# Block 1 of a two-block transformer kernel: rotation moved into the projection, gates into the attention's stage, chunk states scanned in another order, outputs normalised tile by tile

## The chip, the cores and the metric

The kernel runs on one core of one Trainium2 chip. The metric is the device time of one execution in microseconds (us). The engines are called TensorE (PE), VectorE (DVE), ScalarE (ACT), GpSimd (POOL) and SyncE (SP), as in the profile. PE has a clock with two levels, 1.2 and 2.4 GHz; the profile gives the granted clock as a share of the higher one.

## The reference, cut to what matters

The program computes two transformer blocks over 512 latent and 256 context tokens, width 1024, all in float32. Only the token mixer of the first block is touched:

```
q_l = apply_axial_rope(dq_l); k_l = apply_axial_rope(dk_l)
a_l = softmax(q1 k1) v - lam * softmax(q2 k2) v          # 4 heads, differential attention
a_l = rms_norm(a_l, da_subln_g) * (1 - lambda_init)
g_f, g_b = log_gate(lowrank, w2, b)                       # log_sigmoid(...) / 16
# gated linear attention, chunks of 64 tokens, forward and backward:
new_state = state * exp(b_last) + k_to_end^T v
o = (q_dec k_inv^T, masked) v + q_dec state
g_l = rms_norm(o_l, gla_norm_g) * silu(gr_l)
y_lat = concat(a_l, g_l) @ w_out
```

Beside that, the kernel turns the conditioning vectors of all three layers (block 1 and the two layers of block 2) from rows into columns; the later stages need them as columns and, through DRAM, as rows.

## The kernel before

Each engine has its own instruction stream, written by hand. The streams meet at fences: `fence(eng, n)` drains the engine, adds one to the semaphore `stage_done`, and waits until PE, ACT, DVE and POOL have all arrived. SP is not one of the four; it waits for a stage number where it needs one. What lies between two fences is called a stage. The stages of the first block are, in this order:

1. first (loads, modulation of layer 0), 2. `norm1`, 3. `lin1` (the input projection), 4. the modulation's turn and the rotation, 5. attention with its RMS norm, 6. gates, 7. decays (`dec`), 8. states, 9. `glao` (outputs of the linear attention and their norm), 10. `turn` (128x128 transposes), 11. `lin` with `w_out`, 12. norm, 13. routing, then the experts.

**Stage 3, `lin1`.** The weight matrix comes in half blocks x = 0..11 of 512 columns by 512 rows. For each x, ACT rounds the half block to its high part (`act_split1`), DVE makes the low part (`dve_split1`, L590), and PE multiplies four or six token tiles, three matmuls per product. The results are evacuated into `pjt` in turn by ACT and DVE (L715, L718). Columns `DQ` and `DK` (the attention's q and k) are done at x = 3, `GR` (the output gate) comes last, x = 10 and 11. Between the tiles PE works on the modulation of the three layers (L279), DVE copies these out (`dve_mod`, L290), and ACT writes them to DRAM and waits for it (`act_mod`, L298).

**Stage 4.** PE, DVE and ACT turn the modulation (`pe_mod_turn`, `dve_mod_turn` L319 and L326, `act_mod_turn` L331 to L333; ACT waits for its writes to land). Then `dve_da_before` sets two rows to one (L1046), rotates q and k of the four latent tiles, 16 heads of 64 at a time (`dve_rope`, L993 to L998), and sums the products for lambda; ACT takes their exp and DVE makes `lam`. At the same time POOL writes 4 MB of zeros to `ybuf` (L3082) and waits for them to land, and SP loads `x` (2 MB) and `w_out` (4 MB) for stage 11.

**Stage 5.** The attention has 16 units (4 heads by 4 query tiles) in a pipeline over PE, ACT and DVE. After the last one DVE runs `rms_heads`: sums of squares for four tiles, one square root on ACT (L1039), then the scaling by 1/rms and by the gain (L1030, L1035).

**Stage 6.** PE multiplies the low-rank gates by `w2a` (L1091, 33 rows), ACT does Abs, Exp and Ln (L1097, L1100, L1103) and DVE takes `min(x, 0)` minus that (L1110).

**Stage 8.** PE makes the contribution of each of the 12 chunks (chunk 0 to 11), ACT and DVE evacuate them alternately (L1231, L1233), and when all are out DVE scans them, 11 steps of 4 instructions (L1242), forward in the order 8, 9, 10, 11, 0, ..., 7 and backward in 11, 10, 9, 8, 7, ..., 0.

**Stage 9.** For each of four latent tiles PE makes the scores (L1261), DVE masks them (L1295), PE multiplies them by the values and adds the states' part (L1273, L1281), ACT evacuates (L1310). After the fourth tile `rms_heads` runs for all four, ACT takes the Silu of `GR` (L1313), and DVE multiplies by it (L1303).

Of the kernel before, what the change touches and what calls it, by code (L numbers as in the profile page):

```python
# [109 lines left out]
def program(nc, I, out):  # L110
    ctx = ExitStack()
    with ctx:
# [60 lines left out]
        t1_a, t1_v, hi1_a, hi1_v = sem("t1_a"), sem("t1_v"), sem("hi1_a"), sem("hi1_v")  # L173
        w2z, x_again = sem("w2z"), sem("x_again")
# [131 lines left out]
        def pe_mod_turn(pe, layers):  # L306

            for l in layers:
                pe.wait_ge(modr_in[l], 16)
                nc.tensor.transpose(bank(l, 96), modr[0:96, P * l:P * l + P], ident[0:96, 0:96]).then_inc(modT_done, 1)  # L310
            for l in layers:
                pe.wait_ge(modc_ok, l + 1)
                nc.tensor.transpose(bank(3 + l, P)[0:96, :], modc[:, l, :], ident).then_inc(modT_done, 1)

        def dve_mod_turn(dve, layers):
            for i, l in enumerate(layers):
                dve.wait_ge(modT_done, 2 * layers[0] + i + 1)
                b = cols[:, R_MB + 48 * l:R_MB + 48 * l + 48].unsqueeze(1).broadcast_to([P, 2, 48])
                nc.vector.tensor_tensor(modc[:, l, :].rearrange("p (w n) -> p w n", w=2), bank(l, 96).rearrange("p (w n) -> p w n", w=2),  # L319
                                        b, ALU.add).then_inc(modc_ok, 1)  # L320
                dve.drain()
# [6 lines left out]
        def act_mod_turn(act, layers):  # L328
            for i, l in enumerate(layers):
                act.wait_ge(modT_done, 2 * layers[0] + len(layers) + i + 1)  # L330
                act.activation(modr[0:96, P * l:P * l + P], bank(3 + l, P)[0:96, :], ACT.Copy).then_inc(modb_ok, 1)  # L331
                act.wait_ge(modb_ok, l + 1)
                act.dma_start(modd[l].rearrange("w (s q) -> (w s) q", q=P), modr[0:96, P * l:P * l + P]).then_inc(modd_in, 16)  # L333
            act.wait_ge(modd_in, 16 * (layers[-1] + 1))
# [287 lines left out]

        def act_lin1(act, n, p):
            q = 0
            for x in range(N1):
# [13 lines left out]
        def dve_lin1(dve, n, p):  # L639
            q = 0  # L640
            for x in range(N1):
                j, half = x // 2, x % 2
                for m, t in enumerate(BL1[j][2]):
# [9 lines left out]
            nc.vector.tensor_copy(lrt[1][0:32, :], bank(33 % 6, 256)[0:32, :]).then_inc(evac_v, 1)  # L653

# [389 lines left out]
        def dve_da_before(dve):  # L1044
            for r in lrt:
                nc.vector.memset(r[32:33, :], 1.0)  # L1046

            dve.wait_ge(prm, 16 * 7)
            for t in LAT:
                dve_rope(dve, t, hv(DQ, 16, 64)(t), 16, 16, C_R1C, C_R1S, Z[:, 2048 * (t % 2):2048 * (t % 2) + 1024],  # L1050
                         Z[:, 2048 * (t % 2) + 1024:2048 * (t % 2) + 2048])
            l4 = lamt.rearrange("p (a b d) -> p a b d", a=2, b=2)
            pr = Z[:, 9000:9128].rearrange("p (a d) -> p a d", a=2)
# [39 lines left out]
        def act_gates(act, n):  # L1093
# [4 lines left out]
            act.drain()  # L1098
            for b in range(2):
# [106 lines left out]

        def plan_st(n):
            return Plan(n, "av" * 6)

        def pe_states(pe, n):  # L1210
            p = plan_st(n)
            for ci in range(12):
                t, c = ci // 2, ci % 2
                if ci >= 8:
                    pe.wait_ge(EV[p.own[ci - 8]], p.val[ci - 8])
                rs = slice(64 * c, 64 * c + 64)
                for d in range(2):
                    for h in range(4):
                        last = nc.tensor.matmul(bank(ci % 8)[64 * (h % 2):64 * (h % 2) + 64, 256 * d + 128 * (h // 2):256 * d + 128 * (h // 2) + 128],
# [4 lines left out]
        def each_states(eng, n, who):  # L1224
            p = plan_st(n)
            for ci in range(12):
                if p.own[ci] == who:
                    eng.wait_ge(mm_done, p.done(ci))
                    dst = Z[:, 512 * ci:512 * ci + 512]
                    if who == "a":  # L1230
                        nc.scalar.activation(dst, bank(ci % 8), ACT.Copy).then_inc(evac_a, 1)  # L1231
                    else:
                        nc.vector.tensor_copy(dst, bank(ci % 8)).then_inc(evac_v, 1)  # L1233
            if who == "v":
                eng.wait_ge(evac_a, p.val[10])
                eng.drain()
                for s in range(1, 12):
                    for d, order in enumerate((FWD, BWD)):
                        a, b = order[s - 1], order[s]
                        for q in range(2):  # L1240
                            k = 8 * (b // 2) + 4 * d + 2 * q + b % 2
                            nc.vector.scalar_tensor_tensor(DD[:, b, d, q, :], DD[:, a, d, q, :], dec[:, k:k + 1], DD[:, b, d, q, :],  # L1242
                                                           ALU.mult, ALU.add)
                    eng.drain()
# [40 lines left out]

        def dve_glao(dve, n):
            p = plan_o(n)
            for t in range(TL):
# [1973 lines left out]
```

## Time and profile before

| what | value |
|---|---|
| time, median of 3 runs | 4025.27 us (4022.03 to 4025.39) |
| the profiled execution | 4030.13 us, span 4028.2 us |
| PE / DVE / ACT / POOL busy | 3414.9 / 1570.6 / 1107.3 / 647.8 us |
| stages 4 to 10, from the span's start | 325 to 575.5 us |

The profile is of one execution. Times are from the start of its span; an instruction's row gives start, duration, engine, line and operands, and in brackets the idle time of its engine before it and what ended that. "L221" is the fence.

### The profile page before, as it was taken

What the parts mean: (1) busy time and instruction counts of PE and PEld (TensorE: products, weight loads), DVE (VectorE), ACT (ScalarE), POOL (GpSimd) and SP (SyncE); (2) the same over time, 40 slices, a digit from 0 to 9 for tenths busy, and PEclk for the clock granted to TensorE, in tenths of its full rate; (3) what the DMA queues carried; (4) which work ended last, traced back from release to release, by engine and by line L of the source; (5) the groups of instructions that cost most, each with busy time, mean ns of one, the idle gap of its engine ahead of it and who ended that gap; (6) DMA issues with size and microseconds to landing.
All of it is one profiled execution on the core that took longest, in us unless ns stands there. A gap on an engine that the chain in (4) does not pass through costs nothing.

```text
span 4028.2 us, 41123 instructions
## 1 busy us (share of the span) xinstructions
PE 3414.9 (85%) x16083; PEld 2352.7 (58%) x16083; DVE 1570.6 (39%) x2654; ACT 1107.3 (27%) x1925; POOL 647.8 (16%) x471
## 2 busy tenths in 40 slices
PE   4996765787882998788999799999599888988998
PEld 2664543222231884445886488888485456856886
DVE  3226642000004356563333433333474563425444
ACT  3112411112112225443221222221234543303221
POOL 1000001000003325122220100000245223401000
PEclk8998876889996999899999899999799999998999
DMA  6883022799995311002112211111521002233222
GB/s 257 334 314 128 1 105 65 304 427 428 428 429 195 100 44 22 9 1 84 63 63 94 94 63 63 63 63 50 176 81 33 9 35 101 85 110 120 89 93 79
DMA packets 159784, 534.00 MB, mean 133 GB/s; under 512 B 9532, under 2 KB 64724, under 8 KB 136572
## 3 DMA queue, kind: packets, MB, share of 16 engines
q1 hardware_dynamic: 136252, 401.04, 26.9%
q0 software_dynamic: 16880, 92.26, 6.6%
q10 hardware_dynamic: 6480, 38.34, 2.4%
q8 instruction: 116, 1.90, 0.2%
q14 instruction: 56, 0.46, 0.0%
HBM read 488.84 MB, written 42.78 MB: 132 GB/s over the span
## 4 chain that ended last, share of the span: by engine, by line
PE 59%; DVE 4%; ACT 2%; DVEq 1%; DMA 1%; issue 1%; POOL 0%; ACTq 0%; POOLq 0%
PE ps L2774 11%; PE ps L2780 11%; PE ps L1840 7%; PE ps L1842 7%; PE ps L1841 7%; PE ps L511 5%; PE ps L2053 4%; PE ps L2105 2%; PE ps L2093 2%; PE ps L2087 1%; DVE Z L2677 1%; DMA ring<-in_w_out_dram 1%; DVE small L2193 0%; DVE hT_hi L2681 0%; DMA xl<-xspill 0%
## 5 line engine op out<-in xcount | busy, mean ns | idle before, releaser
L2774 PE MATMUL ps<-hT_hi,w_hi 128*128 128x512 f32 (+1 forms) x768 | 275.6, 359 | 27.9 <-DVE w_lo L2828 27.9
L2774 PE MATMUL ps<-hT_hi,w_lo 128*128 128x512 f32 (+1 forms) x768 | 276.4, 360 | 0.0
L2774 PE MATMUL ps<-hT_lo,w_hi 128*128 128x512 f32 (+1 forms) x768 | 275.8, 359 | 0.0
L1840 PE MATMUL ps<-wp_hi,hT_hi 128*128 128x512 f32 (+2 forms) x608 | 222.6, 366 | 37.2 <-POOL wp_lo L1819 37.2
L2780 PE MATMUL ps<-w_hi,h_hi 128*128 128x512 f32 x640 | 253.7, 396 | 0.0
L2780 PE MATMUL ps<-w_hi,h_lo 128*128 128x512 f32 x640 | 253.7, 396 | 0.0
L2780 PE MATMUL ps<-w_lo,h_hi 128*128 128x512 f32 x640 | 253.6, 396 | 0.0
L2053 PE MATMUL ps<-Z 64*128 64x256 f32 (+3 forms) x576 | 202.1, 548 | 28.2 <-DVE small L2195 12.5
L2493 POOL TENSOR_TENSOR mr_lo<-ring,wm_hi 128x2048 fp32r<-128x2048 f32 x36 | 170.7, 4754 | 312.1 <-ACT wm_hi L2485 312.0
L1842 PE MATMUL ps<-wp_hi,hm_lo 128*128 128x512 f32 (+2 forms) x608 | 220.8, 363 | 0.0
L1841 PE MATMUL ps<-wp_lo,hT_hi 128*128 128x512 f32 (+2 forms) x608 | 220.2, 362 | 0.0
L1840 PE MATMUL ps<-wm_hi,hT_hi 128*128 128x512 f32 x480 | 192.6, 401 | 28.3 <-POOL mr_lo L2493 28.3
L2797 ACT ACTIVATE w_hi<-ring 128x2048 fp32r<-128x2048 f32 x64 | 121.9, 1908 | 336.1 <-PE ps L2780 326.7
L511 PE MATMUL ps<-ring,hT 128*128 128x512 f32 x448 | 197.6, 604 | 10.3 <-DMA ring<-in_w_out_dram 9.5
L1605 PE MATMUL ps<-ring,Z 128*64 128x512 f32 x512 | 146.2, 736 | 55.4 <-ACT Z L1627 55.4
L1841 PE MATMUL ps<-mr_lo,hT_hi 128*128 128x512 f32 x480 | 190.7, 397 | 0.0
L1842 PE MATMUL ps<-wm_hi,hm_lo 128*128 128x512 f32 x480 | 190.7, 397 | 0.0
L2828 DVE TENSOR_TENSOR w_lo<-ring,w_hi 128x2048 fp32r<-128x2048 f32 x64 | 146.5, 2292 | 79.9 <-ACT w_hi L2797 79.9
L2774 PEld LDWEIGHTS ps<-hT_hi,w_hi 128*128 128x128 f32 x768 | 145.0, 189 | 52.0 <-issue 28.3
L2850 DVE TENSOR_TENSOR pj<-pj,ps 128x512 f32<-128x512 f32 x140 | 95.5, 686 | 195.0 <-PE ps L2780 195.0
L2774 PEld LDWEIGHTS ps<-hT_lo,w_hi 128*128 128x128 f32 x768 | 145.1, 189 | 24.8
L2774 PEld LDWEIGHTS ps<-hT_hi,w_lo 128*128 128x128 f32 x768 | 145.7, 190 | 23.1
(443 smaller groups left out, 6492.7 us busy)
## 6 DMA issues: line engine op xcount, KB each, us to landing
pj<-in_expert_w_up_dram SPq DMA_DIRECT2D x32, 2048.0 KB, 18.3
pj<-in_expert_w_down_dram SPq DMA_DIRECT2D x32, 2048.0 KB, 19.7
ring<-in_expert_w_gate_dram SPq DMA_DIRECT2D x32, 2048.0 KB, 15.9
ring<-in_ffn_w_dram SPq DMA_DIRECT2D x64, 1024.0 KB, 5.2
ring<-in_w_in_dram SPq DMA_DIRECT2D x58, 1024.0 KB, 5.3
Z<-in_w_mod_dram POOLq DMA_DIRECT2D x24, 2048.0 KB, 8.1
Z<-in_w_ada_dram POOLq DMA_DIRECT2D x8, 2048.0 KB, 9.0
ring<-in_w_out_dram SPq DMA_DIRECT2D x6, 2048.0 KB, 16.2
```

The source lines that it names most:

```text
L511: last = nc.tensor.matmul(bank(i % nb, w), lhs(k, t), s[:, k * w:k * w + w], start=(k == 0), stop=(k == nk - 1))
L1605: last = nc.tensor.matmul(bank(2 + m)[64 * x:64 * x + 64, :], xgT[:, k, 64 * x:64 * x + 64], mslot[2 * m + x][:, 512 * k:512 * k + 512], s ...
L1840: nc.tensor.matmul(out_, a_hi, b_hi, start=first, stop=False)
L1841: nc.tensor.matmul(out_, a_hi, b_lo, start=False, stop=False)
L1842: return nc.tensor.matmul(out_, a_lo, b_hi, start=False, stop=final)
L2053: return nc.tensor.matmul(A.lat(u, x) if k0 == 0 else A.ctx(u, x), S["kq"](p, x, "q")[rs, P * t:P * t + P], S["kq"](p, x, "k")[rs, P * k0: ...
L2493: pool.tensor_tensor(mr_lo[:, 2048 * (x % 4):2048 * (x % 4) + 2048], mring[x % 4], wm_hi[:, 2048 * (x % 3):2048 * (x % 3) + 2048], ALU.sub ...
L2774: last = nc.tensor.matmul(bank(i % 8, c1 - c0), W[a][:, k, :], r[:, k, c0:c1], start=(k == 0 and r is hhk and a == 0), stop=(k == KT - 1 a ...
L2780: last = nc.tensor.matmul(bank(i % 8), H1[hb % 2][a][:, k, P * what:P * what + P], W[b][:, k, :], start=(k == 0 and a == b), stop=(k == 3 ...
L2797: act.activation(WHI[x % 2], raw[x % 4], ACT.Copy).then_inc(w_hi_ok, 1)
L2828: nc.vector.tensor_tensor(WLO[x % 2], raw[x % 4], WHI[x % 2], ALU.subtract).then_inc(w_lo_ok, 1)
L2850: nc.vector.tensor_tensor(y, y, bank(i % 8), ALU.add).then_inc(out_read, 1)
```

## The change

- `dve_rope` for the four tiles is called inside `dve_lin1`, before half blocks x = 4, 5, 6 and 8, as two calls of 8 heads (q, then k); the scratch is the still unused `GR` columns. The products for lambda are summed at the start of `dve_lin1`, ACT's exp is at the start of `act_lin1`, the two rows of ones and `lam` come at the end of `dve_lin1`. Stage 4 as such is gone.
- The modulation's turn and the gates come behind the attention in one stage. On PE the order is attention, gates, turn; on ACT attention, six Abs, the norm's square root, Exp, Ln, turn; on DVE attention, norm, turn, gates. The turn uses one bank each way. ACT no longer waits there for its writes; it waits before it loads the gate row in the `turn` stage.
- The chunks' contributions are made in the order 8, 11, 9, 10, 0, 7, 1, 6, 2, 5, 3, 4, all evacuated by ACT; each scan step waits only for the chunks that it needs. ACT takes Silu of `GR` at the end of that stage.
- POOL multiplies Silu(`GR`) by the gain, one tile per instruction, in the `glao` stage. DVE normalises tile t-1 there after it has masked tile t, with a square root on ACT for each tile.
- POOL's zeros to `ybuf` stay between the third and the fourth fence, now beside the attention. Two fences fewer; the waits of SP on a stage number follow.

```diff
         def dve_lin1(dve, n, p):
             q = 0
+            dve.wait_ge(prm, 16 * 7)
+            dve_lambda_sums(dve)
             for x in range(N1):
                 j, half = x // 2, x % 2
+                if x in ROPE_AT:
+                    if x == ROPE_AT[0]:
+                        dve.wait_ge(evac_a, p.val[8])
+                        dve.drain()
+                    t = ROPE_AT.index(x)
+                    for i, c in enumerate((DQ, DK)):
+                        dve_rope(dve, t, hv(c, 8, 64)(t), 8, 16, C_R1C, C_R1S, pjt[:, 2 * i, GR:GR + 512], pjt[:, 2 * i + 1, GR:GR + 512])
+                    dve.drain()
...
+            for r in lrt:
+                nc.vector.memset(r[32:33, :], 1.0)
+            dve_lambda(dve, n)
...
                 act.activation(sp_[:, t, :], bank(t), ACT.Abs)
             act.drain()
+            rms_heads(act, "a", n, LAT, hv(DQ, 4, 128), 4, 128, subln)
...
+        def dve_states(dve, n):
+            p = plan_st(n)
+            for s in range(1, 12):
+                dve.wait_ge(evac_a, p.val[max(ORD.index(c) for k in range(s + 1) for c in (FWD[k], BWD[k]))])
...
+        def pool_glao(pool):
+
+            for t in LAT:
+                g = hv(GR, 4, 128)(t)
+                pool.tensor_tensor(g, g, glag.unsqueeze(1).broadcast_to([P, 4, 128]), ALU.mult).then_inc(grg_ok, 1)
...
+            def norm(t):
+                v = hv(DK, 4, 128)(t)
+                sq = Z[:, 8192 + 512 * (t % 2):8704 + 512 * (t % 2)].rearrange("p (h d) -> p h d", h=4)
+                ss, vv, sd, rr = (st[:, a + 4 * t:a + 4 * t + 4] for a in (200, 260, 320, 380))
+                dve.wait_ge(evac_a, p.val[6 * t + 5])
+                V.tensor_tensor(sq, v, v, ALU.mult)
+                dve.drain()
+                V.tensor_reduce(ss, sq, AX, ALU.add)
+                dve.drain()
+                V.tensor_scalar(vv, ss, 1.0 / 128, EPS, ALU.mult, ALU.add).then_inc(var, 1)
+                n["std"] += 1
+                dve.wait_ge(std, n["std"])
+                V.reciprocal(rr, sd)
+                dve.drain()
+                V.tensor_tensor(v, v, rr.unsqueeze(2).broadcast_to([P, 4, 128]), ALU.mult)
+                dve.drain()
+                dve.wait_ge(grg_ok, t + 1)
+                V.tensor_tensor(v, v, hv(GR, 4, 128)(t), ALU.mult)
...
             pe_lin1(pe, n)
             fence(pe, n)
-            pe_mod_turn(pe, (0, 1, 2))
-            fence(pe, n)
             pe_attn(pe, n, *da_spec())
-            fence(pe, n)
             pe_gates(pe, n)
+            pe_mod_turn(pe)
             fence(pe, n)
...
             fence(act, n)
+            act.wait_ge(modd_in, 16 * 3)
             load_gate(act, 0, 2)
```

## Rows read from the trace of the kernel before

**Rows 1.** Stretches: their length, busy time of each engine, PE's clock, DMA share.

```profile
core 0: us, PE busy (x) PEld busy (x) DVE busy (x) ACT busy (x) POOL busy (x), PEclk, DMA share, GB/s
72.00:325.00 253.00, 252.23 (x1328) 159.07 (x1328) 59.65 (x68) 32.02 (x35) 22.97 (x32) 0.99 0.81 305
325.00:352.40 27.40, 1.41 (x6) 0.66 (x6) 17.52 (x36) 2.19 (x5) 5.20 (x9) 0.54 0.98 369
352.40:364.80 12.40, 8.93 (x22) 5.23 (x23) 4.70 (x8) 2.77 (x5) 0.00 (x0) 0.50 0.11 43
364.80:447.10 82.30, 76.84 (x436) 57.61 (x434) 72.82 (x149) 41.40 (x84) 0.00 (x0) 1.00 0.00 1
...
459.00:470.00 11.00, 10.60 (x12) 3.83 (x12) 0.00 (x0) 3.30 (x6) 0.00 (x0) 0.50 0.00 0
...
569.00:575.50 6.50, 5.68 (x32) 5.44 (x32) 2.77 (x4) 2.39 (x4) 0.00 (x0) 0.68 0.47 161
```

**Rows 2.** Waits, 324 to 576 us: total, times, longest.

```profile
PE ps L781 <- ACTq L221: 25.0, 1, 25.0
...
DVE Z L960 <- POOLq L221: 7.2, 1, 7.2
```

**Rows 3.** Timeline, DVE at the end of stage 3 and in stage 4.

```profile
324.52 0.41 DVE L653 COPY pj<-ps 32x256 f32<-32x256 f32 x1 [5.61 <-PE ps L1842]
...
325.44 0.26 DVE L319 TENSOR_TENSOR small<-ps,small 128x96 f32<-128x96 f32 x1 [0.51 <-PE ps L310]
...
325.79 0.40 DVE L326 SCALAR_TENSOR_TENSOR small<-small 128x8 f32<-128x8 f32 x4
...
327.65 0.76 DVE L1046 MEMSET pj<- 1x512 f32 x2
328.42 1.22 DVE L993 TENSOR_TENSOR Z<-pj,consts 128x1024 f32<-128x1024 f32 x1
```

**Rows 4.** Timeline, DVE inside the projection.

```profile
165.44 2.79 DVE L290 COPY Z<-ps 2x512 f32<-2x512 f32 x4 [12.40 <-PE ps L279]
...
178.62 0.69 DVE L718 COPY pj<-ps 128x512 f32<-128x512 f32 x1 [0.36 <-PE ps L1842]
...
218.24 2.29 DVE L590 TENSOR_TENSOR w_lo<-ring,w_hi 128x2048 fp32r<-128x2048 f32 x1 [9.21 <-ACT w_hi L582]
```

**Rows 5.** Timeline, end of the attention and the gates, all engines.

```profile
445.45 1.58 PE L832 MATMUL ps<-pj,Z 128*128 128x128 f32 x12 [0.48 <-DVE pj L953]
...
453.07 0.21 ACT L1039 ACTIVATE small<-small 128x16 f32<-128x16 f32 x1 [7.72 <-DVE small L1020]
...
456.47 2.50 DVE L1035 TENSOR_TENSOR pj<-pj,Z 128x512 f32<-128x512 f32 x4
...
469.69 0.60 ACT L1097 ACTIVATE Z<-ps 128x512 f32<-128x512 f32 x1 [1.11 <-PE ps L1091]
470.34 1.28 ACT L1100 ACT_TABLE_LOAD   x1
...
475.84 2.86 ACT L1103 ACTIVATE Z<-Z 128x1536 f32<-128x1536 f32 x2
477.44 3.42 DVE L1110 SCALAR_TENSOR_TENSOR Z<-ps,Z 128x1536 f32<-128x1536 f32 x2 [18.47 <-ACT Z L1103]
```

**Rows 6.** Timeline, DVE in the states and output stages.

```profile
509.90 0.69 DVE L1233 COPY Z<-ps 128x512 f32<-128x512 f32 x1 [1.08 <-PE ps L1219]
...
515.55 13.27 DVE L1242 SCALAR_TENSOR_TENSOR Z<-Z,small 128x128 f32<-128x128 f32 x44
...
543.44 1.42 DVE L1295 TENSOR_TENSOR Z<-ps,consts 128x256 f32<-128x256 f32 x4 [4.28 <-PE ps L1261]
...
554.83 0.69 DVE L1016 TENSOR_TENSOR Z<-pj 128x512 f32<-128x512 f32 x1 [4.28 <-ACT pj L1310]
...
566.36 2.50 DVE L1303 TENSOR_TENSOR pj<-pj 128x512 f32<-128x512 f32 x4
```

**Rows 7.** Groups by line and shape, up to 1300 us: busy us, mean ns.

```profile
L690 POOL TENSOR_TENSOR hm_lo<-pj,hT_hi 128x512 fp32r<-128x512 f32 x8 | 11.5, 1453 | 52.0 <-ACT hT_hi L682 51.3 <-DVE hT_hi L703 0.7
```

More of the change, by code:

```diff
@@ L326, in dve_mod_turn, with act_mod_turn @@
                         nc.vector.scalar_tensor_tensor(Ac[:, l, w, m, :], s, 1.0, g, ALU.add, ALU.mult)
[L328 to L332, printed above, removed]
+        def act_mod_turn(act):
+            act.wait_ge(modT_done, 2)
+            act.activation(modr[0:96, :], bank(6, 3 * P)[0:96, :], ACT.Copy).then_inc(modb_ok, 1)
+            act.wait_ge(modb_ok, 1)
+            for l in range(3):
                 act.dma_start(modd[l].rearrange("w (s q) -> (w s) q", q=P), modr[0:96, P * l:P * l + P]).then_inc(modd_in, 16)
-            act.wait_ge(modd_in, 16 * (layers[-1] + 1))
         def sp_first(sp):
@@ L1222, in pe_states, with act_states @@
                 last.then_inc(mm_done, 1)
-        def each_states(eng, n, who):
+        def act_states(act, n):
             p = plan_st(n)
[L1226 to L1244, printed above, removed]
+            for i, ci in enumerate(ORD):
+                act.wait_ge(mm_done, p.done(i))
+                act.activation(Z[:, 512 * ci:512 * ci + 512], bank(i % 8), ACT.Copy).then_inc(evac_a, 1)
+            act.activation(pjt[:, 0:TL, GR:GR + 512], pjt[:, 0:TL, GR:GR + 512], ACT.Silu)
+        def dve_states(dve, n):
+            p = plan_st(n)
+            for s in range(1, 12):
+                dve.wait_ge(evac_a, p.val[max(ORD.index(c) for k in range(s + 1) for c in (FWD[k], BWD[k]))])
+                for d, order in enumerate((FWD, BWD)):
+                    a, b = order[s - 1], order[s]
+                    for q in range(2):
+                        k = 8 * (b // 2) + 4 * d + 2 * q + b % 2
+                        nc.vector.scalar_tensor_tensor(DD[:, b, d, q, :], DD[:, a, d, q, :], dec[:, k:k + 1], DD[:, b, d, q, :],
+                                                       ALU.mult, ALU.add)
+                dve.drain()
         def plan_o(n):
@@ L3083, in _ @@
             pool.wait_ge(ybz, 16 * (NBLK - NE) * CAP // P)
-            for _ in range(6):
+            for _ in range(3):
                 fence(pool, n)
-            for _ in range(2):
+            pool_glao(pool)
+            for _ in range(3):
                 fence(pool, n)
@@ L3158, in _ @@
             fence(act, n)
[L3159 to L3161 removed]
             act_attn(act, n, *da_spec())
[L3163 to L3164 removed]
             act_gates(act, n)
+            act_mod_turn(act)
             fence(act, n)
```

100 lines of the change are left out of this document (46 added, 54 removed).

## The prediction, made before the changed kernel was run

> **What bounds the kernel now.** I read the page's forty slices first: PE is 85% busy over the whole span, but its slices between 300 and 600 us are weaker. The change touches only block 1, so I split that part into its stages with the view of stretches [rows 1]. The projection (72 to 325 us) is PE's: 252.23 of 253.00 us busy at a clock of 0.99; DVE is busy for 59.65 us of it, ACT for 32.02. The reader should see there that DVE has some 190 us to spare, and that nothing gained on DVE or ACT in that stage can shorten it. From 325 to 575.5 us it is the reverse: PE idles whole stages away, and each stage ends with whichever of the four streams reaches the fence last. In the 27.4 us of stage 4, PE is busy for 1.41, and the DMA engines for 0.98 of the time.
>
> The view of waits names who came last there [rows 2]: PE stood 25.0 us before the attention; DVE, which had finished its rotation at about 345 us, stood another 7.2 us and was let go by POOL's arrival. POOL was waiting for its 4 MB of zeros, which shared the DMA engines with SP's 6 MB. So stage 4 has two limits one behind the other: DVE's rotation until 352.4 - 7.2 = 345.2, the burst until 352.4. Removing the rotation alone would have brought nothing: the burst ends last. It counts that the change also lets POOL wait beside the attention.
>
> **The change part by part.** All numbers are in us, of the profiled execution.
>
> *Stage 4 removed.* Before, the projection's last copy ended at 324.52 + 0.41 = 324.93 [rows 3] and the attention began at 352.4. Now the two memsets (0.76, [rows 3]) and one tiny operation for `lam` follow the copy, with drains about 0.3 more. The attention begins at 326.1: gain 26.3. Bounds 25.5 to 26.6, according to how the memsets overlap.
>
> The rotation costs nothing only while DVE's idle time in the projection covers it. One tile took four instructions, the first of 1024 columns at 1.22 [rows 3], in all three times that width, 3.7. In two calls of half the width the columns are the same and the fixed parts double: a product of 512 columns takes 0.69 [rows 6] against half of 1.22, so eight instructions and their drains make about 4.5 per tile; 3.7 and 5.5 are the bounds. The places: before x = 4 DVE has 12.40 idle, before x = 6 it has 9.21 [rows 4], and x = 8 is like x = 4. Before x = 5 there are only 0.36 [rows 4], so there the evacuation at 178.62 slips to about 183. Who waits for it? PE asks for that bank six tiles later, in half block x = 6, over 10 us on; the next copy comes two tiles later, more than the delay, so it is caught up. Behind a late DVE stand the low parts of the weights (L590), and the next of them comes only when x = 5 is through. Cost 0. If all this cover were missing it would be 4 x 4.5 = 18. The lambda sums wait for parameters loaded in the first microseconds and cost ACT one exp and a table load where it is idle; 0.
>
> The zeros, `x` and `w_out` move nowhere in time, but they now run beside the attention's first 25 us. Nobody in that stage needs them, and the attention lasts about 95, so they land with 65 to spare.
>
> *Start of the attention.* PE ran 8.93 busy us of the first 12.4 at 0.50 [rows 1], having stood 25.0 before. Now it stands about 1.6. At full clock up to 4.5 of the 8.93 would go, but the first 5 us are short transposes between DVE's memsets and copies, so the clock may well fall before the scores come, as it fell in stage 4 (mean 0.54). I take 1.0; bounds 0 and 3.5.
>
> *Gates in the attention's stage.* Before: PE's last value product ended at 445.45 + 1.58 = 447.03, the square root was done at 453.28, the norm at 458.97, PE then did twelve gate passes in 10.60 at a clock of 0.50, the last Abs ended at 470.29, ACT needed from 470.34 to 478.70 (8.36) for two table loads, Exp and Ln, DVE ended at 480.86 [rows 1, 5], and the next stage began at 480.9. Now PE goes on at 447.05 with the gates. At the clock of 1.00 they take 5.3, at 0.50 10.6. These passes use 33 rows, and in their 10.60 us the clock never rose from 0.50 [rows 1], whereas in the attention it rose to 1.00 after 12; so it may fall underway. I take an end at 453.0 (bounds 452.3 and 457.7). The last Abs ends at 453.65. The square root needs a table load (1.28, the duration of L1100's, [rows 5]) that before was hidden behind DVE's sums; now it can start only after the Abs: done at 455.2, where before it was 453.28. That is the new wait: DVE's norm stands 1.9 longer. Norm ends 5.69 later, 460.9. The turn on DVE is three additions (0.26 each) and twelve small products (0.40 for four) [rows 3], with a drain 1.9: 462.8. ACT meanwhile: 455.2 + 8.36 = 463.6, its first half 1.4 earlier, 462.2. So DVE's gates start when DVE is free, 462.8, and take 3.42: 466.2. ACT's copy and three DMA issues after 463.6 fit before that. Next stage at 466.3: gain 480.9 - 466.3 = 14.6. With PE cold throughout, the square root is done at 459.9, Ln at 468.2, DVE at 470.9: gain 10.0. With PE at full clock 15.3.
>
> Here a rule speaks against the change. The trace shows the load itself, 1.28, and Exp starting 1.30 after the load did [rows 5]. ScalarE: Activation LUTs of the Trainium skill (What ACT_TABLE_LOAD costs) counts about 2.66 us for every switch, a drain of 1.38 included. By that rule the square root would come 1.4 later and the gain of this stage would be 13.2. By the rows it is 14.6, and the sum goes by these.
>
> *Decays* (481 to 505): the same instructions after a similar pause of PE; 0.
>
> *States.* Before, DVE began its scan at 515.55 after twelve evacuations; it took 13.27 for 11 steps [rows 6], 1.21 each. The fourth chunk's product was ready at 509.90 [rows 6]. Now the first three steps need chunks 8, 11, 9, 10, the first four made. ACT has the fourth out at about 510.5, so the scan runs 510.6 to 523.9. Step 4 (at 514.2) needs the sixth chunk, out near 513; step 7 (at 517.9) needs the last, out near 515.4. No step waits. ACT's Silu, about 3.2 with its table load, ends near 518.6, inside the scan. Gain 5.0; bounds 3.5 (ACT alone falls 1.5 behind) and 5.2.
>
> *Outputs.* Before, tile by tile PE set the pace: masks 1.42 and DVE's idle time before them 4.28, 5.70 per tile [rows 6]. One tile's norm is now in that gap: square, reduce, scaling and product at 0.69 each, 2.76, the root on ACT 0.21 [rows 5], and about 0.8 for mean, reciprocal and the drains between, together 3.8. It fits with 0.4 to 0.5 to spare. After the last tile, DVE had 554.83 to 568.86 of tail [rows 6]; now only that tile's 3.8 is left: 558.6. Gain 10.2. If each norm were 1.3 too long (a table load each time), three tiles would slip 0.8: gain 7.8. POOL's four products at 1.45 each [rows 7] are done 5.8 after the stage began, and the first is wanted 12 after.
>
> *Turn.* PE ran its transposes at 0.68 [rows 1] after standing 15. It now stands 4.7. Bounds 0 and 2; I take 0.3.
>
> **Sum.** 26.3 + 1.0 + 14.6 + 0 + 5.0 + 10.2 + 0.3 = 57.4. Everything after stage 10 is released by stage numbers, so it moves along; the two fences that go are in the terms. From the profiled 4030.1 this gives 3972.7. The median of the runs lies 4.8 below the profiled one: 4025.3 - 57.4 = 3968.
>
> **The rivals.**
>
> *PE cold through the gates.* For it: 33-row passes did not raise the clock. Against: PE comes from dense work at 1.00. Gain 52.8, time 3972.5.
>
> *The norm does not fit between the masks.* For it: only half a microsecond to spare. If POOL's products ran late and held up the norm's operations, one or two lengths of 1.45 in each of the first two tiles would be 3 to 5: time 3972. Against: POOL's products last into 535, and the first norm starts at 543.44 - 4.28 = 539.2 [rows 6]. This is the case of a rule in SBUF — State Buffer of the Trainium skill (Who interferes with whom): a DVE instruction with two SBUF inputs and a GpSimd instruction that reads SBUF exclude each other for their whole length.
>
> *The burst slows the attention.* For it: 10 MB at a DMA share of 0.98 for 25 us now falls on working engines. Against: the projection ran at a DMA share of 0.81 with PE at its pace [rows 1]. If the attention ran at half pace in that time, 13 would be lost: 3981.
>
> *The rotation is not covered.* If all four tiles show: 18 lost, 3986. Against: the idle times in rows 4.
>
> *Slower than before.* One mechanism: DVE, late by the rotation, lets PE run dry in the projection, and PE's clock falls to 0.50, as it did in stage 4. The price is half of the stretch that PE spends at 0.50. It eats the whole 57.4 when that stretch passes 115 of the projection's 253 us, and shows as slower beyond 131. Four gaps would hardly keep PE at 0.50 for more than 40.
>
> *No effect*: the gain is given back later, by transfers that come by absolute time. I found none; the expert weights start at stage numbers.
>
> **How the numbers follow.** Forecast 0.68 (its own range 3962 to 3974), cold gates 0.12, the norm 0.06, the burst 0.05, the rotation uncovered 0.05, slower 0.02, no effect 0.02. The sum of the terms' low ends is 25.5 + 0 + 10.0 + 3.5 + 7.8 + 0 = 46.8 (3978.5), of the high ends 26.6 + 3.5 + 15.3 + 5.2 + 10.2 + 2 = 62.8 (3962.5). With 2 for the spread of runs and half of the burst's case, the range is 3960 to 3981. A change of 0.2% is 8 us, about what a measurement of this kernel can tell from none; all cases but the last two are beyond it. Faster 0.96, same 0.02, slower 0.02.
>
> **What would show it.** The attention's first transpose at 326 to 327, L718 near 183 with PE's busy share in the projection unchanged; the scores at 0.50 for the first ten microseconds; the square root about 2 after DVE's mean, with a table load before it; the next stage about 113 after the attention's start; the scan beginning 5.5 after PE's first chunk and ending last in its stage; masks still 5.7 apart, one norm after the last. It is wrong if PE shows idle time in the projection, if masks are more than 6 apart, or if later stages lengthen.

## The result and the profile after the change

The changed kernel takes 3979.31 us (median of 4 runs, 3976.24 to 3981.97) against 4025.33 us (4 runs, 4022.03 to 4032.21). The ratio is 0.9879, with a 95% interval of 0.9864 to 0.9894; the medians are 46.0 us apart, and their own quotient, 0.9886, lies in that interval. Its profiled execution took 3981.97 us, span 3980.2; the spans of the two profiles differ by 48.0, and that is what the stages below are added up to.

I cut both traces at the same events: the projection's last copy, the first memset of the attention, the end of its last values product, and PE's first instruction of each later stage. First the stretches of the kernel before (length, then busy time of PE, PE's weight load, DVE, ACT and POOL, then PE's clock):

```profile
324.52:352.57 28.05, 1.57 (x7) 0.82 (x8) 17.93 (x37) 2.19 (x5) 5.20 (x9) 0.55 0.97 363
447.03:480.94 33.91, 10.60 (x12) 3.83 (x13) 14.44 (x22) 12.07 (x13) 0.00 (x0) 0.55 0.00 0
480.94:505.12 24.18, 21.87 (x129) 18.77 (x129) 11.28 (x18) 13.23 (x24) 0.00 (x0) 0.92 0.00 1
505.12:528.95 23.83, 9.58 (x192) 9.34 (x193) 16.67 (x50) 3.58 (x6) 0.00 (x0) 0.64 0.00 1
528.95:568.94 39.99, 20.79 (x256) 17.24 (x257) 18.91 (x38) 7.33 (x12) 0.00 (x0) 0.76 0.00 1
568.94:575.51 6.57, 5.74 (x32) 5.50 (x32) 2.77 (x4) 2.39 (x4) 0.00 (x0) 0.68 0.47 160
```

The same view of the attention before:

```profile
352.57:447.03 94.46, 85.61 (x456) 62.67 (x456) 77.49 (x155) 44.17 (x89) 0.00 (x0) 0.93 0.02 6
```

And the stretches of the changed kernel, the projection and the attention with them:

```profile
72.00:323.00 251.00, 250.10 (x1328) 157.56 (x1326) 75.39 (x100) 32.80 (x37) 22.42 (x32) 0.99 0.82 307
323.31:325.66 2.35, 0.22 (x2) 0.22 (x3) 1.32 (x4) 0.00 (x0) 0.21 (x1) 1.00 0.00 0
325.66:420.11 94.45, 84.57 (x457) 62.04 (x455) 77.47 (x155) 42.88 (x88) 4.99 (x9) 0.95 0.30 112
420.11:441.30 21.19, 9.40 (x19) 3.63 (x19) 15.95 (x37) 13.73 (x15) 0.00 (x0) 0.56 0.03 8
441.30:467.00 25.70, 24.14 (x128) 20.75 (x128) 11.37 (x18) 13.33 (x24) 0.00 (x0) 0.83 0.00 1
467.00:489.82 22.82, 16.02 (x192) 15.62 (x192) 12.53 (x44) 10.36 (x14) 0.00 (x0) 0.50 0.01 1
489.82:520.10 30.28, 21.42 (x256) 17.78 (x257) 17.92 (x40) 4.74 (x13) 4.94 (x4) 0.84 0.00 1
520.10:527.11 7.01, 6.18 (x33) 5.94 (x33) 2.77 (x4) 2.39 (x4) 0.00 (x0) 0.64 0.45 150
```

| stretch | before | after | gain | predicted |
|---|---|---|---|---|
| projection's last copy starts at | 324.52 | 323.31 | 1.2 | none |
| from that copy to the attention | 28.05 | 2.35 | 25.7 | 26.3 |
| attention | 94.46 | 94.45 | 0.0 | 1.0 |
| norm, gates, turn of the modulation | 33.91 | 21.19 | 12.7 | 14.6 |
| decays | 24.18 | 25.70 | -1.5 | 0 |
| states | 23.83 | 22.82 | 1.0 | 5.0 |
| outputs | 39.99 | 30.28 | 9.7 | 10.2 |
| turn | 6.57 | 7.01 | -0.4 | 0.3 |
| all that follows | 3452.7 | 3453.1 | -0.4 | 0 |
| sum | | | 48.0 | 57.4 |

What to see: the two large terms of the sum came as they were worked out; the states gave a fifth of theirs; and the clock column is lower after the change in decays (0.83 for 0.92) and states (0.50 for 0.64).

The trace counts two matmuls for each product that the program writes: its 96 products of the states stage are the 192 matmuls of the rows, 16 for each chunk. The text counts as the trace does.

**The start of the attention**, timeline of the changed kernel, all engines; it answers to [rows 3]:

```profile
323.31 0.41 DVE L669 COPY pj<-ps 32x256 f32<-32x256 f32 x1 [5.61 <-PE ps L1878]
323.88 0.76 DVE L671 MEMSET pj<- 1x512 f32 x2 [0.16 <-issue]
...
325.44 0.66 PE L800 MATMUL ps<-consts,pj 128*128 128x128 f32 x4 [2.17 <-DVEq L222]
```

PE stands 2.17 where it stood 25.0 [rows 2]. The rotation now lies in the projection; DVE's timeline there, before half block x = 5, shows the end of a tile and the copy that it delays; it answers to [rows 4]:

```profile
180.45 0.69 DVE L1017 TENSOR_TENSOR pj<-pj 128x512 f32<-128x512 f32 x1
181.21 0.69 DVE L737 COPY pj<-ps 128x512 f32<-128x512 f32 x1
```

This tile began at 176.98, so one tile takes 4.2, and the copy comes at 181.21, where it was 178.62. PE is busy for 250.10 of 251.00 us at 0.99. Its only wait in that stretch, 0.9, is for a DMA and lies before the first rotated tile, and from 150 to 323 us it is busy throughout: it did not wait for that copy.

**Norm and gates**, timeline of all engines; it answers to [rows 5]:

```profile
420.04 7.92 PE L1103 MATMUL ps<-Z,pj 33*128 33x512 f32 x12
...
428.00 0.60 ACT L1109 ACTIVATE Z<-ps 128x512 f32<-128x512 f32 x1 [1.11 <-PE ps L1103]
428.93 1.28 ACT L1058 ACT_TABLE_LOAD   x1 [0.34 <-issue]
430.22 0.22 ACT L1058 ACTIVATE small<-small 128x16 f32<-128x16 f32 x1
...
430.47 0.25 DVE L1042 RECIPROCAL small<-small 128x16 f32<-128x16 f32 x1 [4.35 <-ACT small L1058]
```

The last Abs starts at 428.00, behind twelve gate passes that took 7.92 and not 5.95. The root stands behind it, and DVE waits 4.35 for the root, where it waited 0.28 before the change: that is the new wait, 4.1 longer where 1.9 was forecast.

**States**, timeline of ACT and DVE; it answers to [rows 6]:

```profile
467.00 16.02 PE L1234 MATMUL ps<-pj 64*64 64x128 f32 x192 [0.33 <-ACTq L222]
469.08 0.60 ACT L1243 ACTIVATE Z<-ps 128x512 f32<-128x512 f32 x1 [2.17 <-PE ps L1234]
469.94 0.60 ACT L1243 ACTIVATE Z<-ps 128x512 f32<-128x512 f32 x1 [0.26 <-PE ps L1234]
471.65 0.60 ACT L1243 ACTIVATE Z<-ps 128x512 f32<-128x512 f32 x1 [1.11 <-PE ps L1234]
472.57 0.60 ACT L1243 ACTIVATE Z<-ps 128x512 f32<-128x512 f32 x1 [0.32 <-PE ps L1234]
473.27 4.79 DVE L1254 SCALAR_TENSOR_TENSOR Z<-Z,small 128x128 f32<-128x128 f32 x16 [11.71 <-ACT Z L1243]
...
478.45 1.14 DVE L1254 SCALAR_TENSOR_TENSOR Z<-Z,small 128x128 f32<-128x128 f32 x4 [0.38 <-ACT Z L1243]
...
481.08 1.14 DVE L1254 SCALAR_TENSOR_TENSOR Z<-Z,small 128x128 f32<-128x128 f32 x4 [1.49 <-ACT Z L1243]
...
483.70 5.99 DVE L1254 SCALAR_TENSOR_TENSOR Z<-Z,small 128x128 f32<-128x128 f32 x20 [1.49 <-ACT Z L1243]
```

ACT is never the slow one: each of its evacuations waits for PE. They come 0.86, 1.71, 0.92 apart, and then 1.71 and 0.92 in turn to the last. The scan, which was to run through, stops three times (0.38, 1.49, 1.49) and begins 6.27 after PE's first product, not 5.5. The same 192 products take 16.02 where they took 9.58.

**Outputs**, timeline of POOL, then of DVE; it answers to [rows 6]:

```profile
489.86 4.94 POOL L1302 TENSOR_TENSOR pj<-pj,Z 128x512 f32<-128x512 f32 x4 [158.91 <-DVEq L222]
```

```profile
504.94 1.42 DVE L1334 TENSOR_TENSOR Z<-ps,consts 128x256 f32<-128x256 f32 x4 [0.69 <-PE ps L1273]
...
510.64 1.42 DVE L1334 TENSOR_TENSOR Z<-ps,consts 128x256 f32<-128x256 f32 x4 [0.69 <-PE ps L1273]
...
516.34 0.69 DVE L1313 TENSOR_TENSOR Z<-pj 128x512 f32<-128x512 f32 x1 [0.69 <-ACT pj L1345]
```

The masks stay 5.70 apart with 0.69 to spare, and one norm follows the last. POOL has ended at 494.80, and DVE's first norm begins at 500.58.

### The profile page after: what moved, and what is told of

Same layout as the page of the kernel before. It is cut to its first block, busy times and chain, and to the rows that moved or that the text cites. A ratio compares the mean times of both kernels' runs of the same rounds, so it can differ in the third digit from the quotient of the medians.

```text
span 3980.2 us, 41148 instructions
## 1 busy us (share of the span) xinstructions
PE 3421.7 (86%) x16083; PEld 2357.8 (59%) x16083; DVE 1562.5 (39%) x2666; ACT 1108.8 (28%) x1931; POOL 651.7 (16%) x475
## 4 chain that ended last, share of the span: by engine, by line
PE 59%; DVE 5%; ACT 2%; DVEq 1%; DMA 1%; issue 1%; POOL 1%; ACTq 0%; POOLq 0%
PE ps L2810 11%; PE ps L2816 11%; PE ps L1876 7%; PE ps L1878 7%; PE ps L1877 7%; PE ps L514 5%; PE ps L2089 4%; PE ps L2141 2%; PE ps L2129 2%; PE ps L2123 1%; DVE small L2229 1%; DVE Z L2713 1%; DMA ring<-in_w_out_dram 1%; DVEq L222 1%; DVE hT_hi L2717 0%
```

## The experiments

Ten runs. "Changed kernel" is the one of the result; each edit is against it unless it says otherwise.

**1. The order of the chunks.** Chunk c uses rows 0 to 63 of the array when c is even and 64 to 127 when it is odd. The changed order puts two chunks of one half side by side 5 times in 11 (11 and 9, 10 and 0, 7 and 1, 6 and 2, 5 and 3); the order of before never does. This edit keeps what the scan needs and lets the halves alternate.

```diff
-        ORD = [8, 11, 9, 10, 0, 7, 1, 6, 2, 5, 3, 4]
+        ORD = [8, 11, 10, 9, 0, 7, 6, 1, 2, 5, 4, 3]
```

> The changed kernel with one list changed: the chunks are made in the order 8, 11, 10, 9, 0, 7, 6, 1, 2, 5, 4, 3, so that neighbours always lie in different halves of a token tile (even and odd chunk numbers). Theory A (array halves): a chunk's products use only 64 of the array's rows, neighbours in different halves overlap on PE, neighbours in the same half do not; in the changed kernel 5 of 11 neighbours share a half, and those evacuations came 1.71 us apart against 0.86 to 0.92 for the others. Expected: all evacuations 0.9 us apart or closer, PE's 192 products in 9.6 to 11 us instead of 16.0, the scan's 11 steps without waits once begun, the states stage 18.5 to 20 us instead of 22.8, the time 3 to 4 us shorter than the changed kernel's, about 3975.5. Rival B (clock): PE's products took 16 us because the clock stayed at 0.50; the order has nothing to do with it, the stage stays at 22 to 23 us.

Measured: 3974.83 us (3973.18 to 3976.36, 4 runs), ratio to the kernel before 0.9867 (0.9850 to 0.9883). The states stage, stretch view and then timeline:

```profile
463.84:482.66 18.82, 8.63 (x193) 8.39 (x193) 12.52 (x44) 9.55 (x14) 0.00 (x0) 0.68 0.01 2
```

```profile
465.92 0.60 ACT L1243 ACTIVATE Z<-ps 128x512 f32<-128x512 f32 x1 [2.17 <-PE ps L1234]
466.78 0.60 ACT L1243 ACTIVATE Z<-ps 128x512 f32<-128x512 f32 x1 [0.26 <-PE ps L1234]
467.70 0.60 ACT L1243 ACTIVATE Z<-ps 128x512 f32<-128x512 f32 x1 [0.32 <-PE ps L1234]
```

Read them against those of the changed kernel: 0.86 and 0.92 apart, no 1.71. The stage is 4.0 shorter (22.82 to 18.82), 5.0 shorter than before: the gain that was forecast. The scan began 5.41 after PE's first matmul (469.25) and ran its 44 instructions in 13.28 without a wait.

Two things changed on PE. Its 192 matmuls took 8.63 for 16.02; five pairs at 0.79 are 4.0 of these 7.4, and the rest is the clock: here it stood at 0.50 up to the third evacuation (467.70) and then rose, a mean of 0.90 from there to 470.50 and 1.00 behind that; in the changed kernel it never rose. The time of the whole kernel can't settle a step of this size: the interval of its ratio overlaps that of the changed kernel. The gain is read from the stage.

**2. The same order in the kernel before**, where two engines evacuate. It separates the array's halves from ACT's doing all the evacuations. The edit is in the kernel before; the banks and the turns of ACT and DVE follow the new order, all else stays:

```diff
+        ORD = [8, 11, 9, 10, 0, 7, 1, 6, 2, 5, 3, 4]
...
-            for ci in range(12):
+            for i, ci in enumerate(ORD):
```

> The kernel before, with only the order in which the chunks are made changed to 8, 11, 9, 10, 0, 7, 1, 6, 2, 5, 3, 4; ACT and DVE still evacuate alternately and the scan still waits for all. Theory A (array halves): PE's 192 products take about 16 us instead of 9.6, because 5 of 11 neighbours share a half, and the stage becomes 29 to 31 us instead of 23.8; the time is about 6 us longer than before, about 4031. Rival B (ACT alone): the slow products came from leaving all twelve evacuations to ACT; with two engines evacuating the order costs nothing, stage 23 to 25 us.

Measured: 4037.04 us (4027.27 to 4038.89, 8 runs) against 4028.85 (13 runs); the medians are 8.2 apart, the ratio of 1.0014 (1.0004 to 1.0024) is 5.6 us. Stretch view of its states stage, then ACT's timeline there:

```profile
504.93:535.20 30.27, 16.02 (x193) 15.62 (x193) 16.67 (x50) 3.58 (x6) 0.00 (x0) 0.50 0.00 1
```

```profile
507.00 0.60 ACT L1233 ACTIVATE Z<-ps 128x512 f32<-128x512 f32 x1 [2.16 <-PE ps L1221]
509.57 0.60 ACT L1233 ACTIVATE Z<-ps 128x512 f32<-128x512 f32 x1 [1.97 <-PE ps L1221]
```

ACT takes every second chunk here: 2.57 for the first two, which is 0.86 + 1.71 again, then 2.63 for every two, which is 0.92 + 1.71, and PE's 16.02 again. The order alone makes this stage 6.4 longer (30.27 for 23.83). So the pace is PE's, and comes from the order; who evacuates has no part in it.

**3. The norm's root ahead of the six Abs.**

```diff
         def act_gates(act, n):
             p = plan_gate(n)
+            rms_heads(act, "a", n, LAT, hv(DQ, 4, 128), 4, 128, subln)
             for t in range(TA):
...
-            rms_heads(act, "a", n, LAT, hv(DQ, 4, 128), 4, 128, subln)
```

> The changed kernel with ACT's square root for the attention's norm ahead of the six Abs. Theory A: the root came 4.4 us late because the Abs stand before it on ACT and need PE's gate passes; ahead of them it is done 0.5 us after DVE's mean, as before the change, the norm on DVE ends about 3.9 us earlier, and the six Abs follow back to back (3 us) so that Exp begins about 0.8 us earlier. DVE's last gate operation then waits for Ln instead of for the norm: the next stage begins 1 to 2 us earlier, the time is about 3978. Rival B: ACT's chain of table loads, Exp and Ln is the whole path and the root only shifts inside it; the stage stays within 0.3 us of what it was.

Measured: 3981.59 us (3973.07 to 3985.05, 4 runs), ratio 0.9885 (0.9869 to 0.9902), beside the changed kernel's 0.9879. ACT's timeline:

```profile
418.18 1.28 ACT L1058 ACT_TABLE_LOAD   x1
427.18 0.22 ACT L1058 ACTIVATE small<-small 128x16 f32<-128x16 f32 x1 [7.72 <-DVE small L1039]
427.30 3.02 ACT L1110 ACTIVATE Z<-ps 128x512 f32<-128x512 f32 x6
```

The load is hidden again, 9 us ahead of the root. But the six Abs now queue behind the root and end at 430.32. The stage took 19.75 with gate passes of 7.9, 1.4 less than the 21.19. With fast passes it gives nothing and costs something: with both edits (passes 5.54) it took 19.76, with the order alone (5.87) 19.14, and in the changed kernel's second execution (experiment 9, 5.41) 18.7. The time shows no gain.

**4. Both edits together.** The two diffs above.

> The changed kernel with both edits, the alternating chunk order and ACT's square root ahead of the Abs. Theory A: they act in different stages and add up, 4.0 us from the order (always) and 0 to 1.5 us from the root, depending on how long PE's clock stays up in the gate passes (the root's place matters only when these passes run at 0.50): about 3974.5, states stage 18.8 us, attention's last value product to the next stage 19.7 us in every execution. Rival B: the root's new place costs up to 0.9 us where the clock stays up, and the sum is no better than the order alone, 3975 or more.

Measured: 3976.38 us (3971.35 to 3977.30, 4 runs), ratio 0.9873 (0.9856 to 0.9889): not better than the order alone, as rival B says. Its states stage took 18.69.

**5. The burst awaited.** PE waits for the zeros before the attention.

```diff
             fence(pe, n)
+            pe.wait_ge(ybz, 16 * (NBLK - NE) * CAP // P)
             pe_attn(pe, n, *da_spec())
```

> The changed kernel with one wait added: PE waits for POOL's 4 MB of zeros before the attention. Theory A (two limits in stage 4): the burst of 10 MB alone held the attention until 27 us after the projection, so this one wait brings nearly all of stage 4 back: attention at 350 to 352 us, time 25 to 27 us longer, about 4005. Rival B: the burst ended so late only because other work of stage 4 delayed it or ran beside it; without that work it lands earlier and the wait costs 15 us or less, about 3994.

Measured: 4002.80 us (2 runs, 4000.33 to 4005.27), 23.5 more than the changed kernel, a little less than the 25 to 27 of theory A. PE's timeline:

```profile
349.65 1.09 PE L800 MATMUL ps<-consts,pj 128*128 128x128 f32 x4 [26.21 <-DMA ybuf<-hT]
```

PE starts 24.2 later than with the change. The burst alone, with no rotation anywhere near it, restores nearly the whole of the old stage.

**6. The rotation after the projection**, where it stood, with the burst still beside the attention.

```diff
-        ROPE_AT = (4, 5, 6, 8)
+        ROPE_AT = ()
...
+            dve.wait_ge(evac_a, p.val[8])
+            dve.drain()
+            for t in LAT:
+                dve_rope(dve, t, hv(DQ, 16, 64)(t), 16, 16, C_R1C, C_R1S, Z[:, 2048 * (t % 2):2048 * (t % 2) + 1024],
+                         Z[:, 2048 * (t % 2) + 1024:2048 * (t % 2) + 2048])
+            dve.drain()
             for r in lrt:
```

> The changed kernel with the rotation of the four tiles (16 heads at a time, as before the change) put behind the projection's last evacuation instead of inside the projection; POOL's zeros stay beside the attention. Theory A: the rotation alone is worth its DVE time, four tiles at 3.6 us, so the attention begins 14.5 to 15.5 us later and the time is about 3994. Rival B: the rotation was covered by the burst anyway and costs nothing where it is: within 2 us of the changed kernel.

Measured: 3995.79 us (2 runs, 3995.17 to 3996.41), 16.5 more. PE's timeline:

```profile
340.81 1.12 PE L806 MATMUL ps<-consts,pj 128*128 128x128 f32 x4 [16.45 <-DVEq L222]
```

PE starts 15.4 later than with the change. The two prices, 24.2 and 15.4, add up to 39.6, far more than the 25.7 that leaving both away gave: the two run at the same time, and the one that ends first is hidden behind the other.

**7. The norms after the last tile.** The four norms of the outputs' stage run together at its end, as before.

```diff
-                if t:
-                    norm(t - 1)
-            norm(TL - 1)
+            for t in range(TL):
+                norm(t)
```

> The changed kernel with the four tiles' norms one after the other behind the last tile instead of between the masks. Theory A: a norm between masks is free, so taking all four behind costs three norms of 3.7 us: the output stage 41 to 42 us instead of 30.3, time about 3990 to 3992. Rival B: the norms between the masks already slow PE's tiles, so that moving them out gives back 2 us or more: stage 39 us or less.

Measured: 3988.93 us (2 runs, 3986.01 to 3991.85), 9.6 more. PE's timeline, the first instruction of the stage and of the next:

```profile
488.23 2.08 PE L1273 MATMUL ps<-hT 64*128 64x128 f32 x16 [6.79 <-DVEq L222]
...
528.11 5.72 PE L1363 MATMUL ps<-consts,pj 128*128 128x128 f32 x32 [14.86 <-DVEq L222]
```

The stage is 39.88 long, 9.6 more than 30.28 and 0.1 off the 39.99 of before; that lies between the 41 to 42 of theory A and the 39 of rival B. DVE's masks tell the two apart:

```profile
502.64 1.42 DVE L1334 TENSOR_TENSOR Z<-ps,consts 128x256 f32<-128x256 f32 x4 [4.29 <-PE ps L1273]
...
508.34 1.42 DVE L1334 TENSOR_TENSOR Z<-ps,consts 128x256 f32<-128x256 f32 x4 [4.28 <-PE ps L1273]
```

They are 5.70 apart as well, with nothing between them, so the norm between the masks costs nothing.

**8. The two-column products spread.** With the order of experiment 1. At the end of the decays PE made 48 products of two columns each, for all six tiles; here each tile makes its own eight. It tests whether PE's clock falls where these thin products stand in a row. That they leave the array's columns idle, as the expectation has it, no run shows.

```diff
                 if 1 <= t <= TL:
                     turn_dec(pe, n, p, t - 1)
-            for t in range(TA):
                 for d in range(2):
                     for q in range(2):
```

> The alternating order again, and the 48 products of two columns that end the decay stage spread over its six tiles (8 passes behind each tile's own work). Theory A (clock): these products keep the array idle in most of its columns, PE's clock falls to 0.50 at their end and the states stage starts cold; spread out, the states' first four chunks come 0.5 us apart instead of 0.9, PE's 192 products take about 6.5 us instead of 8.6, the scan starts 3 to 4 us after PE, and the states stage is 17 us. The decay stage loses at most what it gains: its end loses 5.4 to 6.7 us, each tile grows by about 0.9. Time 2 to 3 us below the alternating order alone. Rival B: the clock falls at the fence or by chance of the moment, the states stage starts cold as often as before, stage 18.5 to 19 us.

Measured: 3970.03 us (3967.29 to 3971.09, 4 runs), ratio 0.9855 (0.9839 to 0.9872): the lowest median of this study, though the interval still overlaps that of experiment 1 (0.9850 to 0.9883). Stretch view, decays and states:

```profile
439.52:461.95 22.43, 21.64 (x128) 19.05 (x128) 11.36 (x18) 13.34 (x24) 0.00 (x0) 0.91 0.00 1
461.95:478.74 16.79, 6.59 (x193) 6.35 (x193) 12.52 (x44) 9.23 (x14) 0.00 (x0) 0.77 0.01 2
```

Against experiment 1 (25.55 and 18.82) the decays are 3.1 shorter and the states 2.0. The decays scatter without this edit, from 24.2 to 26.9 in ten traces, so the 3.1 is the difference of two executions; 22.4 lies below all ten. The states' products take 6.59 for 8.63, all of them at a clock of 1.00 (461.95 to 468.60), although PE had stood for 0.79 ahead of them; in experiment 1 it had stood for 0.33 and began at 0.50. So the fence, which rival B names, does not by itself bring the clock down. Some comes back: the outputs take 30.83 for 29.38 and the turn 7.34 for 6.22.

**9 and 10. The changed kernel and the spread one again**, unaltered, on one chip.

> The changed kernel once more, with nothing altered, beside the next one on one chip. Theory A (the order of the chunks costs, the moment of PE's clock fall in the gates is scatter): the states stage is 22.8 again with PE's 192 products at 16.0, while the twelve gate passes may come out anywhere between 5.4 and 7.9 and the stage behind the values between 18.7 and 21.2; median near 3979. Theory B (both belong to the kernel): the gate passes are 7.9 and the stage 21.2 again.

> The order with alternating halves and the two-column products spread, once more, beside the unaltered changed kernel on one chip. Theory A (both edits are worth what their stages showed, 6.0 in the states and about 3.3 in the decays, less 1 to 2 given back in the outputs): 7 to 10 below the unaltered kernel's median, states stage 16.8, decays 22.4. Theory B (the earlier difference was the chip or the execution): within 3 of it.

Measured: changed kernel 3980.29 us (3977.74 to 3982.47, 4 runs), ratio 0.9883 (0.9867 to 0.9900); spread 3970.92 (3967.24 to 3974.59, 4 runs), ratio 0.9859 (0.9842 to 0.9875). They differ by 9.4, within the 7 to 10 of theory A, and no run of one lies among those of the other. The spread kernel's stages came again too: decays 22.4, states 16.8, its products 6.59. The changed kernel's second execution, timeline of all engines:

```profile
420.37 5.41 PE L1103 MATMUL ps<-Z,pj 33*128 33x512 f32 x12
...
428.29 0.25 DVE L1042 RECIPROCAL small<-small 128x16 f32<-128x16 f32 x1 [1.84 <-ACT small L1058]
...
439.13 3.35 PE L1139 MATMUL ps<-Z,consts 128*128 128x256 f32 x7 [3.60 <-DVEq L222]
```

The same program, another execution: twelve gate passes in 5.41, DVE's wait for the root 1.84, and from the values' end (420.44) to the next stage 18.7 and not 21.2. But the decays then took 26.9 and not 25.7, since the 48 thin products ran for 8.15 and not 6.74. The states took 22.82 with 16.02 on PE, to the hundredth as in the first. So the order is the kernel's; the moment at which the clock falls is the execution's.

## Why the prediction was right, and where it was off

The time lies in the range, but partly by luck. It is 3979.3 against 3968, a gain of 46.0 against 57.4. That is outside the forecast's own 3962 to 3974, and even 0.8 beyond 3978.5, the sum of all low ends. It falls within 3960 to 3981 only by the allowance for the spread of runs and for a burst that slows the attention, and no such slowing shows. (In the spans of the profiled executions the gain is 48.0, just inside the low ends' 46.8.) None of the rivals happened either: the mechanisms were those of the forecast, except in one step, the states. The misses of the terms, in the spans: states 4.0, gates 1.9, decays 1.5, start of the attention 1.0, turn 0.7, stage 4 0.6, outputs 0.5, and 0.4 behind the changed part, less 1.2 by which this projection happened to end earlier: 9.4 = 57.4 - 48.0. The other 2.0 is the profiled execution's distance to the median, 4.8 before and 2.7 after.

**Stage 4: right.** The two limits, rotation and burst, the earlier hidden behind the later, are shown by experiments 5 and 6 (24.2 and 15.4 for one of them put back), and the early start in the trace. The prediction's point that moving the rotation alone would have brought nothing was not run as a kernel; experiment 5, where the burst alone holds the attention back to 349.65, leaves 25.7 - 24.2 = 1.5 as the gain of moving it and the turn together. The 0.6 that is missing is what follows the memsets: `lam`, the drains and the fence take 0.80 (324.64 to 325.44), more than was counted.

**Rotation in the projection: right.** 4.2 per tile for the 4.5 taken; copy at 181.21 for "about 183"; no wait of PE behind it. This refutes the rival of the uncovered rotation and the one that ended slower. Experiment 6 gives the price of a rotation that shows, 15.4, but for 16 heads at a time; the 18 was worked out for the two calls of 8, of which four tiles at the measured 4.2 would be 17.

**Burst beside the attention: right.** The stage takes 94.45 for 94.46, at a DMA share of 0.30 for 0.02. Equal lengths alone could hide a loss behind the gain of the early start, so compare the part behind PE's third group of transposes: 90.7 with the burst beside it (329.38 to 420.11), 90.7 in experiment 5, where the burst had landed first (352.69 to 443.41), and 90.6 before. That rival falls.

**Start of the attention: 1.0 too much.** PE had stood for 2.17 only, and its first four transposes took 0.66, where they took 1.11 before. But the third group waits for DVE: 2.10 now, 1.34 before, and it starts 3.94 after the first, as before (4.02), at a clock of 0.50 again. So the stage did not get shorter at all. The step said that it might go so; its lower bound held.

**Gates: the chain right, one term off in this execution.** Passes were taken at 5.95, the profiled execution had 7.92, and of the six executions with the same instructions up to there (the changed kernel's two, experiments 1, 7, 8 and 10) one had 7.92, one 5.87 and four 5.41. In the four others with the gates behind the attention (experiments 3, 4, 5 and 6) they took 7.92, 5.54, 7.35 and 7.56. Where they took 5.87, in experiment 1, the stretch lasted 19.14, a gain of 14.8 against the 14.6 of the sum; and with 5.41 the wait for the root was 1.84, 1.6 longer than the 0.28 of before, against 1.9. The rival "PE cold through the gates" (10.6) did not occur in any. No run put the gates back behind a fence of their own: the 12.7 is read from the two traces, the chain from their rows.

The load ahead of the root started at 428.93 and the root at 430.22: 1.29 for a switch. The prediction set the 2.66 of ScalarE: Activation LUTs in the Trainium skill (What ACT_TABLE_LOAD costs) against that, with 13.2 for the stage. The 12.7 measured looks like it and isn't: it comes from the passes, and no row here shows the extra drain of 1.38.

**Decays: 1.5 worse, and that is scatter as far as the runs show.** Experiment 2, which has none of the change ahead of them, had them at 25.5 for 24.18; experiments 3 and 5, which have the change, at 24.2 and 24.3; the changed kernel's two executions at 25.7 and 26.9. The row of the clock says how: 0.83 for 0.92. What decides the moment at which it falls is not settled.

**States: this step failed**, a gain of 1.0 where 5.0 was forecast with 3.5 as the lower bound. The prediction took from [rows 6] that the fourth chunk's product is ready at 509.90, 4.8 after PE's first, and the last near 515.4, 10.3 after it, whatever the order. Here the fourth was ready 5.6 after it, and the last was out 16.7 after it. The forecast's times hold for an order in which neighbours use opposite halves of the array. Side by side in one half they take 1.71 per chunk, in opposite halves 0.92, both at a clock of 0.50. Five pairs in one half make 5 x 0.79 = 4.0, the whole miss, and experiment 1 gave these 4.0 back. Experiment 2 shows the same 16.02 without any of the change's other parts. On DVE it shows as a scan that begins 0.9 later and stops three times, where "no step waits" was forecast. The clock that stayed at 0.50 costs PE more time on top (16.02 against 9.58 is 6.4, of which the pairs are 4.0), but the stage none, by this estimate: with the pairs gone and the clock still at 0.50, the last chunk would be out 16.67 - 3.95 = 12.7 after PE's first product, which is when the scan of experiment 1 wants it (18.69 - 5.99 = 12.7).

TensorEngine Tiling (Array Packing) of the Trainium skill (Key Properties, under Tiling Modes) says that different tiles can load weights and multiply in parallel, and that each is tied to its partitions. The trace agrees, 0.92 against 1.71, and shows that the two need not be in one group of products: chunk against chunk is enough.

**Outputs: right**, 9.7 for 10.2. The norm fits (5.70 apart, 0.69 to spare), POOL's products took 1.24 each for 1.45, and experiment 7 gives the part its price, 9.6. The conflict of DVE and POOL that the rival rested on does not appear: POOL's four ended 4.94 after the stage began, 5.8 before the first norm, so it was not tried either.

**Left open.** Why the clock falls in one execution in the gates and in another in the thin products. Why the clock does not rise in the 16.02 us of the changed order while it does in the alternating one: all seven traces with the changed order show it, none tells the cause. And whether spreading the thin products shortens the decays by keeping the clock up or by covering their own time. In the states it is the clock: the products, 8.63 to 6.59 with not one of them altered, ran at 1.00 from the start.

**The best version** is that of experiment 8: 9.4 below the changed kernel on one chip, 0.9855 and 0.9859 of the kernel before in its two sets of runs. How much of that is the order and how much the spreading is read from the stages only.

## What to carry to other kernels

Before you reorder matmuls that use half of the array's rows, write down the half of each: two neighbours in one half cost 1.71 where two in opposite halves cost 0.92, and one line of the order decided 4 us. A wait that is taken off a barrier is worth what the next arrival leaves of it: put each one back alone, as in experiments 5 and 6, to see how many there are. And try the thinnest matmuls between others instead of in a row at a stage's end: here their stage took 22.4 where it had taken 24.2 to 26.9, and the next lost 2.0.

## What the runs showed of the hardware that was not expected

- Products of 64 rows by 64 columns in opposite row halves overlap although they belong to different chunks and banks: 16 of them per 0.92 us, against 1.71 in the same half, clock 0.50 in both.
- With the changed order PE stayed at 0.50 through 16.02 us of products without a pause, and the 16.02 came again in experiments 2, 3, 5, 6, 7 and 9; with alternating halves the stage ran at 0.68, and at 0.77 behind the spread products.
- In all ten traces where the thin products stand in a row, PE's clock fell while they ran or right behind them, and the states began at 0.50: in the changed kernel it was 1.00 from 459.93 to 462 and 0.50 from 464, PE busy all the while; in the kernel before it fell in the 0.33 behind them. Spread over the stage, they left it at 1.00 at the end of the decays and through the states' products, in both executions.
- ACT issues a table load ahead of the wait of the activation that needs it: in experiment 3 the load at 418.18, the root at 427.18. That is why a root can hide its load only if nothing else stands between.
- The 3450 us behind the changed part differ between executions by up to 10.5 us with not one instruction of theirs altered: 3446.4 in experiment 3, 3453.1 in the changed kernel, 3456.9 in experiment 10. A difference of under 5 in the medians of this kernel has to be read from its stage.
